# Gated linear attention stage: low-rank gate product in column groups, block exponentials on ScalarE, both directions summed in PSUM, parameters loaded beside the queries

## The reference, cut to what matters

```python
def _c_streams(h, w_in, gate_up, gate_b):
    q, k, v, g, low = _split(h @ w_in, C_WIDTHS)          # low: 2 directions x rank 16
    ...
    log_a = [_heads(jax.nn.log_sigmoid((low[:, :, d] @ gate_up[d] + gate_b[d])) / GATE_TAU, H_C)
             for d in range(2)]

def step(st, inp):                                        # _gla_scan, one chunk
    qc, kc, vc, la = inp
    cum = jnp.cumsum(la, axis=2)
    rel = cum[:, :, :, None, :] - cum[:, :, None, :, :]   # causal part only
    scores = jnp.einsum('bhtk,bhsk,bhtsk->bhts', qc, kc, jnp.exp(rel))
    out = jnp.einsum('bhtk,bhkv->bhtv', qc * jnp.exp(cum), st) + jnp.einsum('bhts,bhsv->bhtv', scores, vc)
    total = cum[:, :, -1:, :]
    st = jnp.exp(total[:, :, 0, :, None]) * st + jnp.einsum('bhsk,bhsv->bhkv', kc * jnp.exp(total - cum), vc)
```

## Time and profile before

| | |
|---|---|
| median of 3 runs | 3726.69 us (3725.66 to 3728.09) |
| the profiled execution's own time | 3727.9 us |
| its span, first to last instruction | 3726.1 us |
| PE busy | 3027.1 us (81%) |
| DVE busy | 1978.5 us (53%) |
| ACT busy | 807.6 us (22%) |
| mean granted TensorE clock | 0.934 |
| the gated linear attention stage | 2004.9 to 2173.6 us of the span, 4.5% |

### The profile page before, as it was taken

One profiled execution on the slowest core, in us unless ns is written; L12 is line 12 of the kernel. 1 busy time (PEld: TensorE's weight loads), 2 busy tenths in 40 slices (PEclk: granted clock), 3 DMA queues, 4 the chain that ended last, 5 costly groups with the idle time before them and its releaser, 6 DMA issues. The chain is left out here.

```text
span 3726.1 us, 28065 instructions
## 1 busy us (share of the span) xinstructions
PE 3027.1 (81%) x8564; PEld 1486.6 (40%) x8564; DVE 1978.5 (53%) x5049; ACT 807.6 (22%) x2034; POOL 876.3 (24%) x772
## 2 busy tenths in 40 slices
PE   7997788888888888777797668888877788897898
PEld 3443443333333333332342434333332545453663
DVE  1136557777777777777700847777776332222100
ACT  0112312222222222222301212222222130121000
POOL 0000004444444444444300003444444000000000
PEclk9997799999999999999998779999999898898999
DMA  5143229999999999999822338999999443333333
GB/s 197 57 151 122 70 97 427 427 427 427 427 427 423 424 421 419 424 421 416 349 77 70 113 136 364 427 427 427 426 427 427 152 147 108 114 113 113 113 139 120
DMA packets 241739, 1023.96 MB, mean 275 GB/s; under 512 B 45494, under 2 KB 50102, under 8 KB 141222
## 3 DMA queue, kind: packets, MB, share of 16 engines
q0 software_dynamic: 110592, 805.36, 51.4%
q1 hardware_dynamic: 130568, 215.55, 16.4%
q10 hardware_dynamic: 432, 1.31, 0.1%
HBM read 1021.02 MB, written 1.13 MB: 274 GB/s over the span
## 5 line engine op out<-in xcount | busy, mean ns | idle before, releaser
L1497 PE MATMUL l_peer_experts_acc<-l_peer_experts_ring,l_peer_experts_diag 128*128 128x512 f32 x1840 | 856.0, 607 | 208.7 <-ACT l_peer_experts_diag L1555 208.2
L1497 PE MATMUL l_peer_experts_acc<-weight_slots,l_peer_experts_diag 128*128 128x512 f32 x1232 | 592.2, 624 | 158.6 <-ACT l_peer_experts_diag L1555 158.2
L1716 DVE SCALAR_TENSOR_TENSOR l_peer_experts_ring<-l_peer_experts_ring,h_tiles 128x1024 f32<-128x1024 f32 x460 | 563.4, 1225 | 274.0 <-DMA l_peer_experts_ring<-in_expert_rows,l_peer_experts_picks 270.3
L1424 POOL DMA_INDIRECT weight_slots<-in_expert_rows,l_peer_experts_picks x308 | 350.8, 1139 | 1406.3 <-DVE l_peer_experts_picks L1645 965.3
L1424 POOL DMA_INDIRECT l_peer_experts_ring<-in_expert_rows,l_peer_experts_picks x460 | 525.4, 1142 | 606.7 <-PE l_peer_experts_acc L1497 533.4
L1497 PEld LDWEIGHTS l_peer_experts_acc<-l_peer_experts_ring,l_peer_experts_diag 128*128 128x128 f32 x1840 | 336.2, 191 | 697.4 <-issue 400.7
L1716 DVE SCALAR_TENSOR_TENSOR weight_slots<-weight_slots,h_tiles 128x1024 f32<-128x1024 f32 x308 | 377.3, 1225 | 187.0 <-DMA weight_slots<-in_expert_rows,l_peer_experts_picks 182.2
L1497 PEld LDWEIGHTS l_peer_experts_acc<-weight_slots,l_peer_experts_diag 128*128 128x128 f32 x1232 | 231.9, 197 | 495.8 <-issue 281.9
L1548 ACT ACTIVATE l_peer_experts_gel<-l_peer_experts_dots 128x2 f32<-128x2 f32 x384 | 78.2, 204 | 1183.8 <-DVE l_peer_experts_ring L1716 708.8
L1555 ACT ACTIVATE l_peer_experts_diag<-const_ident,l_peer_experts_wgt 128x128 f32<-128x128 f32 x768 | 266.3, 394 | 237.7 <-DVE l_peer_experts_wgt L1662 223.2
L1449 PE MATMUL l_peer_experts_queries<-h_t,l_query_weights 128*128 128x512 f32 (+3 forms) x576 | 182.6, 463 | 4.2 <-PEq L61 4.2
(11 more groups left out here) (462 smaller groups left out, 3359.4 us busy)
## 6 DMA issues: line engine op xcount, KB each, us to landing
weight_slots<-in_w_mod SPq DMA_DIRECT2D x24, 2048.0 KB, 7.7
weight_slots<-in_w_in SPq DMA_DIRECT2D x20, 2048.0 KB, 7.5
l_query_weights<-query_weights SPq DMA_DIRECT2D x16, 1024.0 KB
weight_slots<-in_w_mlp_up SPq DMA_DIRECT2D x8, 2048.0 KB, 7.6
weight_slots<-in_w_mlp_down SPq DMA_DIRECT2D x8, 2048.0 KB, 7.6
weight_slots<-in_gla_w_in SPq DMA_DIRECT2D x6, 2048.0 KB, 7.6
weight_slots<-in_ab_w_in SPq DMA_DIRECT2D x5, 2048.0 KB, 8.8
l_peer_experts_ring<-in_expert_rows,l_peer_experts_picks POOLq DMA_INDIRECT x460, 16.7
```

Source lines behind the costliest of these rows:

```text
L1424: pool.indirect_dma_start(rows(b, k, None), None, uv, bass.IndirectOffsetOnAxis(ap=picks[:, b % 4, k:k + 1], axis=0)).then_inc(landing(b, ...
L1497: ins = nc.tensor.matmul(acc[:, b % 2, c * BANK:(c + 1) * BANK], diag[:, k % DIAGS, :], row[:, c * BANK:(c + 1) * BANK], start=(k == 0), s ...
L1716: nc.vector.scalar_tensor_tensor(row, row, 1.0, h[:, tile_of(b), :], ALU.mult, ALU.mult, accum_out=dots[:, b % 2, k:k + 1]).then_inc(dotte ...
```

## The change

- **Low-rank product:** one set of four column groups of 32 columns works at once: two groups hold one half of the contraction each in the order (direction 0, direction 1), two in the order (1, 0); PE adds nothing up, the second product does: `up` now has 128 rows, zero but for 16 in each group. One copy by ACT instead of two.
- **Parameters:** `wl`, `up` and `bias` are loaded by SP in the query stage `c_q`, ahead of its weight load, after a memset of `up` by POOL. SP waits at the stage's end for them.
- **Block exponentials:** the subtractions L1930, L1931 and the caps L1933, L1934 leave DVE. ACT computes exp(scale*cum + bias) for each of 4 sub-blocks of 2 chunks, with the reference as a bias column: 8 instructions of 128x128 and 8 of 128x32 instead of one of 128x1024 and one of 128x256. DVE makes the bias columns (2 instructions of 128x8), and caps in the multiplications.
- **Results:** both directions of a head accumulate in PSUM, in one of two banks, and ACT reads them once per head (128x512), instead of two DVE instructions per unit.
- **Modulation stores:** nobody waits at the end of the three stages; the next user of the row buffers and the head norm's SP wait instead.

```diff
@@ class Modulation, sync @@
+        self.weights.wait_mod_stored(sp)
         bias(0)
         bias(1)
...
-        for s in range(2):
-            sp.wait_ge(self.stored[s], 16 * ((self.tiles + 1 - s) // 2))
@@ stage_linear @@
+            if early:
+                @block.gpsimd
+                def _(pool):
+                    for cleared_one in early[0]:
+                        nc.gpsimd.memset(cleared_one, 0.0).then_inc(cleared, 1)
             @block.sync
             def _(sp):
+                if early:
+                    sp.wait_ge(cleared, len(early[0]))
+                    for dst, src in early[1]:
+                        sp.dma_start(dst, src, allow_slow_non_contiguous=True).then_inc(early_loaded, 16)
...
                     weights.load(sp, i + 2)
+                if early:
+                    sp.wait_ge(early_loaded, 16 * len(early[1]))
@@ stage_head_norm @@
+            if weights:
+                @block.sync
+                def _(sp):
+                    weights.wait_mod_stored(sp)
@@ stage_gla, PE @@
-                pe.wait_ge(loaded, 64)
-                for d in range(2):
-                    for k in range(KC):
-                        last = nc.tensor.matmul(ps_l[0:RANK, d, :], wl[:, k, d * RANK:(d + 1) * RANK], act_t[:, k, 0:TOK],
-                                                start=(k == 0), stop=(k == KC - 1))
-                    last.then_inc(low_done, 1)
-                pe.wait_ge(low_ready, 2)
+                for n in range(KC // 2):
+                    for j in range(4):
+                        cols = wl[:, n + KC // 2 * (j // 2), j % 2:j % 2 + 2, :].rearrange("p d n -> p (d n)")
+                        last = nc.tensor.matmul(ps_l[32 * j:32 * j + 32, 0, :], cols, act_t[:, n + KC // 2 * (j // 2), 0:TOK],
+                                                start=(n == 0), stop=(n == KC // 2 - 1), tile_position=(0, 32 * j))
+                last.then_inc(low_done, 1)
+                pe.wait_ge(low_ready, 1)
...
-                    nc.tensor.matmul(ps_l[:, u % 2, :], up[:, d, h * P:(h + 1) * P], low[:, d, :], start=True, stop=True).then_inc(logit_done, 1)
+                    nc.tensor.matmul(ps_l[:, u % 2, :], up[:, d, h * P:(h + 1) * P], low[:, :], start=True, stop=True).then_inc(logit_done, 1)
...
-                    if u:
-                        pe.wait_ge(out_taken, u)
+                    if d == 0 and h >= 2:
+                        pe.wait_ge(out_taken, h - 1)
@@ stage_gla, ACT @@
-                    nc.scalar.activation(ks[:, b, :, :, :], ks[:, b, :, :, :], ACT.Exp, scale=1.0 / 16.0)
-                    nc.scalar.activation(qs[:, b, :, :, :], qs[:, b, :, :, :], ACT.Exp, scale=1.0 / 16.0)
+                    for c in range(2):
+                        for j in range(NSUB):
+                            cu = cum[:, b3, 2 + c, :]
+                            nc.scalar.activation(ks[:, b, c, j, :], cu, ACT.Exp, scale=-1.0 / 16.0, bias=refs[:, b, 0, c, j:j + 1])
+                            nc.scalar.activation(qs[:, b, c, j, :], cu[:, j * SUB:(j + 1) * SUB], ACT.Exp, scale=1.0 / 16.0, bias=refs[:, b, 1, c, j:j + 1])
...
                 for u in range(n_units - 1):
                     copy_keys(u + 1)
+                    if u and u % 2 == 0:
+                        take_results(u // 2 - 1)
                     if u + 2 < n_units:
                         exponentials(u + 2)
+                take_results(H_C - 1)
@@ stage_gla, DVE @@
-                        nc.vector.tensor_tensor(ks[:, b, c, :, :], ref.to_broadcast([P, NSUB, P]), cu.unsqueeze(1).to_broadcast([P, NSUB, P]), ALU.subtract)
-                        last = nc.vector.tensor_tensor(qs[:, b, c, :, :], cu.rearrange("p (j s) -> p j s", s=SUB), ref.to_broadcast([P, NSUB, SUB]), ALU.subtract)
-                    link(last)
-                    nc.vector.tensor_scalar(ks[:, b, :, :, :], ks[:, b, :, :, :], 16.0 * FAR_CAP, None, ALU.min)
-                    nc.vector.tensor_scalar(qs[:, b, :, :, :], qs[:, b, :, :, :], 16.0 * FAR_CAP, None, ALU.min).then_inc(args_ready, 1)
+                    ref = cum[:, b3, 2:4, :].rearrange("p c (j s) -> p c j s", s=SUB)[:, :, :, SUB // 2]
+                    nc.vector.tensor_scalar(refs[:, b, 0, :, :], ref, 1.0 / 16.0, None, ALU.mult)
+                    nc.vector.tensor_scalar(refs[:, b, 1, :, :], ref, -1.0 / 16.0, QUERY_LOG, ALU.mult, ALU.add).then_inc(args_ready, 1)
...
-                        nc.vector.tensor_tensor(ks[:, b, c, :, :], ks[:, b, c, :, :], kk.unsqueeze(1).to_broadcast([P, NSUB, P]), ALU.mult)
-                        nc.vector.scalar_tensor_tensor(q_sub, q_sub, float(P) ** -0.5, qq, ALU.mult, ALU.mult)
+                        nc.vector.scalar_tensor_tensor(ks[:, b, c, :, :], ks[:, b, c, :, :], math.exp(FAR_CAP), kk.unsqueeze(1).to_broadcast([P, NSUB, P]), ALU.min, ALU.mult)
+                        nc.vector.scalar_tensor_tensor(q_sub, q_sub, math.exp(FAR_CAP + QUERY_LOG), qq, ALU.min, ALU.mult)
...
-                        take_results(u - 1)
@@ mixer_c @@
+            early = [(wl[:, :, 0:2, :].rearrange("p k d n -> p k (d n)"), low_w.rearrange("(k p) n -> p k n", p=P)),
+                     (wl[:, :, 2, :], low_w[:, 0:RANK].rearrange("(k p) n -> p k n", p=P))]
+            early += [(up[32 * j:32 * j + RANK, j % 2, :], up_w[j % 2]) for j in range(4)]
+            early += [(bias[:, d, :], a["gla_gate_b"][0][d].rearrange("(h p) -> p h", p=P)) for d in range(2)]
```

More of the change, by code:

```diff
@@ L120, in begin, with wait_mod_stored @@
             self.load(sp, i)
+    def wait_mod_stored(self, sp):
+        for s in range(2):
+            if self.n_mod_stored[s]:
+                sp.wait_ge(self.mod_stored[s], self.n_mod_stored[s])
     def count(self, i, turn):
@@ L378, with __init__ @@
     PER = KC // GROUPS
-    def __init__(self, nc, st, weights, name, silu_c, bias, mod_rows, first, banks):
+    def __init__(self, nc, st, weights, name, silu_c, bias, mod_rows, rows, first, banks):
         planned, _, n, _ = weights.plan[weights.at]
@@ L390, in __init__ @@
         self.bias_loaded = [st.sem(f"mod_bias_loaded{s}") for s in range(2)]
-        self.stored = [st.sem(f"mod_stored{s}") for s in range(2)]
+        self.stored, self.before = weights.mod_stored, list(weights.n_mod_stored)
         self.link_sem = st.sem("mod_chain")
@@ L466, in sync, with done @@
                 bias(i + 1)
+    def done(self):
         for s in range(2):
[L469 to L471 removed]
+            self.weights.n_mod_stored[s] = self.before[s] + 16 * ((self.tiles + 1 - s) // 2)
         self.weights.n += self.tiles
@@ L1856, in _ @@
                 link = Link(act, achain)
-                for d in range(2):
-                    act.wait_ge(low_done, d + 1)
-                    nc.scalar.activation(low[:, d, :], ps_l[0:RANK, d, :], ACT.Copy).then_inc(low_ready, 1)
+                act.wait_ge(low_done, 1)
+                nc.scalar.activation(low[:, :], ps_l[:, 0, :], ACT.Copy).then_inc(low_ready, 1)
                 for u, (h, d) in enumerate(units):
```

71 lines of the change are left out of this document (29 added, 42 removed).

## The result

The changed kernel takes **3674.8 us** (median of 4 runs, 3672.0 to 3678.7) where the kernel before takes 3727.4 in the same series (median of 4 runs, 3725.7 to 3734.5): a ratio of 0.9856, with a 95% interval of 0.9841 to 0.9870. The profiled execution of it took 3677.0 us, with a span of 3675.2.

The account below looks back on a forecast made before the run. It took the attention loop to be one cycle through VectorE and the modulation matmuls. Terms -20.7 - 17.5 - 2.1 - 4.9 - 1.6 + 0.5 = -46.3 us gave 3680.4 us for the median, range 3671 to 3697.

Parts of the forecast that it names:

- likeliest case: Whole kernel: the prediction's own case, all terms as priced, 3676 to 3686 us, chance 0.47.
- rival 3: Attention stage: better than forecast by a cheap bias column or logits at full clock; 3674 us, chance 0.08.
- Term 1, start to logit: Attention stage start: loads gone and low-rank product in 3.6 us, so logits start 20.7 us earlier.
- Term 1, the logits: Attention stage's logits: they keep 14.5 us; 3.6 better if the clock stayed at 2.4 GHz.
- Term 2: ScalarE's sixteen new exponentials per unit: 4.1 us, with ends of 2.5 and 5.7.
- rival 1: ScalarE: narrow exponentials don't overlap, 5.7 us for sixteen, +12.4 us, total 3693 us; chance 0.2.
- Term 3: Attention loop: ScalarE's cycle of 9.6 us bounds, first to last copy 64.8 us against 82.3, -17.5.
- Rival 2: Attention stage: TensorE stays at 1.2 GHz in low-rank product and loop; total 3689 us, chance 0.2.
- Term 3, the result copies: Loop: result copies on ScalarE, 0.6 us every second unit, hidden in its idle time; 1.8 in all if not.
- Term 4: Run-in to the loop: scores of unit 0 at 2065.0 instead of 2067.13, -2.1 us.
- Term 5: Ends of stages: -4.9 us in this stage, -1.6 at mLSTM's end, +0.5 for the norm's weights.
- Term 6: Query stage: memset and eight loads hide beside its matmuls, 0 us, at worst +3.

Follow-up runs that it names:

- e2: Changed kernel with the low-rank product back in two sets of 16 columns, logits contracting over 16 rows; 3687.9 us, ratio 0.9887.
- e3: As e2, but the logits' matmuls contract over all 128 rows, 112 of them zero; 3688.2 us, ratio 0.9893.
- e1: Changed kernel with the eight parameter loads moved from the query stage back into the gated linear attention stage; 3687.9 us, ratio 0.9886.
- e7: Changed kernel with the log-sigmoid combinations moved earlier, the first ahead of the loop, the second into the first unit; 3680.5 us, ratio 0.9871.
- e5: Changed kernel with the results leaving PSUM by VectorE again, one copy or addition per unit; 3682.5 us, ratio 0.9873.
- e6: Changed kernel with the wait for the modulation stores back at the end of the three stages; 3682.2 us, ratio 0.9880.
- e9: Changed kernel with the queries' exponents subtracted on VectorE and one 128x256 exponential for the eight narrow ones; 3671.6 us, ratio 0.9851.
- e10: Changed kernel with four more 128x32 exponentials per unit on ScalarE, whose results nobody reads; 3681.2 us, ratio 0.9878.
- e4: Changed kernel with the block exponents' subtractions and caps back on VectorE and two wide exponentials on ScalarE; 3688.6 us, ratio 0.9895.
- e8: Changed kernel with the edits of e7 and e9 together; 3667.5 us, ratio 0.9837.

## Why the prediction was right, step by step

The median lies 5.6 us below the forecast of 3680.4, inside the range of 3671 to 3697 and 1.2 below the lower end of the likeliest case, 3676 to 3686. The sign and the mechanisms of the large terms held. What came is that case with one half of rival 3, the logits at full clock (3.4 us), and 3.2 us ahead of the query stage that no term has and that no run gives to the change.

- **Term 1, start to logit:** -20.8 for -20.7. The column groups are worth 10.2 of it (e2, e3). The loads are worth the other 10.6: 7.6 of waiting (2004.91 to 2012.56), and 2.9 because the product behind the wait took 16.83 us where without the wait it takes 13.89 (e2). Putting them back costs 11.8 (e1), more than that, as e1 issues eight loads for four. The full clock was rightly taken.
- **Term 1, the logits:** the step that failed is "the logits themselves keep 14.5 us". Its reason, that the added rows are hidden by the stream over 512 tokens, is right for a matmul's own time (at full clock the first four rows of the trace take 1.98 us before and after) but overlooks the clock: with 128 rows instead of 16 TensorE stays at 2.4 GHz (e2 against e3). The text named the price, 3.6 better; 3.4 was measured. The number of rows was not seen as its cause, so it was given only a part of the 0.08 of rival 3.
- **Term 2:** 4.03 us for 4.1. The ends of its range, 2.5 and 5.7, are both out. Neighbours overlap, so rival 1 falls. The rule of the Trainium skill (ScalarE: Activation LUTs, Rules for kernel authors) describes the single instruction well: about 0.3 us and 0.83 ns an element give 0.41 and 0.33 us by estimate, and the durations are 0.386 and 0.306. Adding it up to 5.9 us for a run of sixteen was the prediction's own step, and that is what the trace disagrees with: each instruction starts 0.09 us before the end of the one ahead of it (0.386 less 0.29, 0.306 less 0.21).
- **Term 3:** -17.8 for -17.5. ScalarE bounds the periods four and five, 9.25 and 9.85 us from copy to copy, with a cycle of 9.39 for 9.6, and the last two periods came as worked out (8.33, 6.94 for 8.4, 7.0). The second and third took 12.94 and 8.32 where 11.9 and 9.6 were predicted, nearly the same together: behind the combination TensorE stood idle for 2.91 us and its matmuls then ran at half clock, which cost 1.66, and while VectorE was held up ScalarE got ahead, so the next period was TensorE's own. Two errors cancel there, and that is luck. That TensorE would keep its full clock behind 1 us of idle time held in the changed kernel, again with some luck: in e7 it fails twice, behind 0.86 and 1.31 us.
- **Rival 2** (TensorE at 1.2 GHz) is rejected for the low-rank product and happened in one period of the loop, and in the run-in (first scores 3.62 us, first modulation set 3.64), which Term 4 had as before.
- **Term 3, the result copies** were put at nothing, hidden in ScalarE's idle time. No run gives them another place on ScalarE; the loop came out 0.2 short of a sum without them, and moving them back to VectorE costs 2.0 (e5), 0.7 without the slower matmuls.
- **Term 4:** -1.8 for -2.1.
- **Term 5:** -4.0 for -4.9 here and -1.7 for -1.6 at the mLSTM stage; e6 gives 3.9 and 1.9 by itself. What was mis-sized is the bare barrier, taken as 2.15 from the attention stage's end and here 2.96 from the store. Why it is longer here was not tried. The norm's weights cost nothing for a predicted +0.5.
- **Term 6:** 0. The eight issues of the query stage took 4.0 us of SP's time, beside 15.4 us of matmuls.
- **Not in the sum:** ahead of the query stage 3.2 us more went than predicted. Of them 2.2 lie ahead of the mLSTM stage's last modulation copy, 1.6 of these between its first and last (74.7 us before, 73.1 after). The windows from 220 to 312 us, before and after:

```profile
220.00:312.00 92.00, 75.44 (x351) 33.89 (x350) 45.57 (x150) 19.48 (x60) 0.00 (x0) 0.87 0.56 202
```

```profile
220.00:312.00 92.00, 71.67 (x354) 34.35 (x352) 47.75 (x156) 20.13 (x62) 0.00 (x0) 0.92 0.58 207
```

The clock is 0.87 and 0.92. With this stage's code as in the changed kernel its eight modulation copies span 73.1 us in some kernels (e2, e3, e7, e9, e10) and 74.6 to 75.0 in others (e1, e4, e5, e8). So the change need not have brought these 1.6 us; what decides which of the two an execution gets is open, and so is the rest of the 3.2.

## What to carry to other kernels

Before pricing a stage with small matmuls, read the granted clock of its window: a contraction over few rows can run at 1.2 GHz where the same matmul with its rows filled, even by zeros, runs at 2.4, and work that keeps TensorE waiting can cost its own length and the clock too, so that two edits together may bring several times what each brings alone (here 6.3 us for 0.7 and 1.4). Price a run of narrow ScalarE instructions by the distance of their starts, not by their durations. When work leaves the bounding engine, name the engine that bounds next and its cycle, since a second relief of the first engine is then worth much less (here 2.0 us instead of 6.5).

## What the runs showed of the hardware that was not expected

- Of eight float32 matmuls of 512 columns and 16 contraction rows all but the first few ran at 1.2 GHz (e2, granted clock 0.54 and then 0.50, 22.9 us to the combination); with 128 rows, 112 of them zero, they ran at 2.4 GHz (e3, 1.00, 19.5 us).
- After 11.7 us of idle time the low-rank product needed 5.19 us instead of 3.64, and the logits behind it still ran at the full clock (e1).
- The same 0.86 us of idle time ahead of a modulation set (eight matmuls) went with 1.92 us for it in one kernel and with 3.46 in another (e7), and the other was never idle for longer in the 20 us before.
- Eight small loads took SP 4.0 us to issue in the query stage and 8.5 in the gated linear attention stage (e1).
